# A transformer chain on one core: attention's and the cell's query and key units strictly in turn, with new program orders in the mixers

## The reference

```
proj = h @ w_in                       # aq ak av | mq mk mv mo | gates
aq = partial_rotary(aq) * 64 ** -0.5  # attention: 8 heads of 64
ak = partial_rotary(ak)
attn = dilated_attention_mixture(aq, ak, av)
qk = silu(depthwise_conv5(mq, mk) + conv_b)   # the cell: 4 heads of 128
cell = mlstm(qk, mv, gates, forwards) + mlstm(qk, mv, gates, backwards)
merged = [attn, sigmoid(mo) * rms(cell)]
out = merged @ w_out
```

## Time and profile before

| | |
|---|---|
| median of 3 runs | 2042.23 us (2041.54 to 2042.46) |
| profiled execution, its own time | 2042.36 us |
| its span, first to last instruction | 2040.5 us |
| granted TensorE clock, mean | 0.999 of full speed |
| busy, of the span: PE, DVE, ACT, POOL | 99%, 83%, 50%, 5% |
| first mixer, window | 1227 to 1358 us |
| second mixer, window | 1721.3 to 1852.2 us |

### The profile page before, as it was taken

The page is one execution under the profiler, slowest core; times in us unless marked ns, Lnnn a source line. Parts: engine busy times, 40 slices in busy tenths (PEclk is TensorE's granted clock), DMA queues, the critical chain, the costliest instruction groups (busy, mean ns, idle before and its releaser), DMA issues.

```text
span 2040.5 us, 26105 instructions
## 1 busy us (share of the span) xinstructions
PE 2027.1 (99%) x9966; PEld 1699.8 (83%) x9966; DVE 1698.7 (83%) x2866; ACT 1017.7 (50%) x1204; POOL 110.1 (5%) x228
## 2 busy tenths in 40 slices
PE   9999999999999999999999999999999999999998
PEld 7888878888988888888888889888888888978887
DVE  7888889887579887888889877989888987889986
ACT  5554445445565444554454445854445444675442
POOL 0010011000010000000010000010001000001000
PEclk9999999999999999999999999999999999999999
DMA  8576655756446556566566657356656755536562
GB/s 286 173 236 226 193 179 191 228 187 207 157 152 212 200 186 207 186 211 201 186 207 219 201 168 225 125 159 216 199 190 206 225 196 185 186 124 196 187 200 88
DMA packets 291166, 393.22 MB, mean 193 GB/s; under 512 B 9941, under 2 KB 257061, under 8 KB 290914
## 3 DMA queue, kind: packets, MB, share of 16 engines
q1 hardware_dynamic: 284176, 368.16, 55.5%
q10 hardware_dynamic: 4034, 14.23, 2.1%
q0 software_dynamic: 2832, 9.17, 1.6%
HBM read 390.44 MB, written 2.12 MB: 192 GB/s over the span
## 4 chain that ended last, share of the span: by engine, by line
PE 95%; DVE 2%; ACT 1%; issue 0%; DMA 0%; SPq 0%; POOL 0%; POOLq 0%; ACTq 0%; DVEq 0%
PE psum L602 26%; PE psum L604 26%; PE psum L603 26%; PE psum L626 4%; PE psum L641 2%; PE psum L646 2%; PE psum L650 2%; PE psum L628 2%; PE psum L735 1%; DVE w_lo L1780 1%; PE psum L780 0%; PE psum L781 0%; PE psum L784 0%; ACT w_hi L1277 0%; PE psum L918 0%
## 5 line engine op out<-in xcount | busy, mean ns | idle before, releaser
L1780 DVE TENSOR_TENSOR w_lo<-raw,w_hi 128x2048 fp32r<-128x2048 f32 x349 | 794.3, 2288 | 109.8 <-ACT w_hi L1277 106.5
L1277 ACT ACTIVATE w_hi<-raw 128x2048 fp32r<-128x2048 f32 x349 | 663.3, 1909 | 120.5 <-PE psum L604 85.3
L602 PE MATMUL psum<-w_hi,xT 128*128 128x512 f32 (+1 forms) x1408 | 545.8, 388 | 0.0
L604 PE MATMUL psum<-w_hi,xT 128*128 128x512 f32 (+1 forms) x1408 | 543.4, 386 | 0.0
L603 PE MATMUL psum<-w_lo,xT 128*128 128x512 f32 (+1 forms) x1408 | 543.3, 386 | 0.0
L1830 DVE STREAM_TRANSPOSE h_turned<-h_full 32x128 f32<-32x128 f32 x1408 | 426.6, 303 | 21.1
L602 PEld LDWEIGHTS psum<-w_hi,xT 128*128 128x128 f32 x1408 | 264.6, 188 | 53.3 <-issue 0.8
L604 PEld LDWEIGHTS psum<-w_hi,xT 128*128 128x128 f32 x1408 | 264.5, 188 | 53.4
L603 PEld LDWEIGHTS psum<-w_lo,xT 128*128 128x128 f32 x1408 | 264.5, 188 | 52.4
L602 PE MATMUL psum<-w_hi,h_hi 128*128 128x512 f32 x768 | 300.0, 391 | 0.0
L604 PE MATMUL psum<-w_hi,h_lo 128*128 128x512 f32 x768 | 299.3, 390 | 0.0
(11 more groups left out here) (255 smaller groups left out, 1916.4 us busy)
## 6 DMA issues: line engine op xcount, KB each, us to landing
raw<-in_ffn_w_in SPq DMA_DIRECT2D x176, 512.0 KB, 4.9
raw<-in_ffn_w_gate SPq DMA_DIRECT2D x88, 512.0 KB, 4.0
raw<-in_ffn_w_up SPq DMA_DIRECT2D x88, 512.0 KB, 5.0
raw<-in_ffn_w_down SPq DMA_DIRECT2D x44, 1024.0 KB, 4.9
raw<-in_ffn_w_out SPq DMA_DIRECT2D x44, 1024.0 KB, 4.9
raw<-in_conv_w_in SPq DMA_DIRECT2D x20, 1024.0 KB, 5.3
raw<-in_mix_w_in SPq DMA_DIRECT2D x16, 1024.0 KB, 5.4
raw<-in_mix_w_in SPq DMA_DIRECT2D x24, 512.0 KB, 4.8
```

Of the source, the lines that this page charges most:

```text
L602: pe.matmul(dst, l_hi, r_hi, start=first, stop=False, skip_group_check=loose)
L604: return pe.matmul(dst, l_lo, r_hi, start=False, stop=last, skip_group_check=loose)
L1277: return act.activation(dst, source, ACT.Copy, **kw)
L1780: dve.tensor_tensor(low(u), raw_of(u), f32(high(u)), ALU.subtract).then_inc(lo_ready, 1)
```

## The change

`MIX_UNITS` now has attention's and the cell's units strictly in turn: aq mk ak mq aq mk ak mq. Loads, tap and rotary tables follow from that list. The programs of TensorE, ScalarE and VectorE in the mixer are the same calls in another order (`first_tap` has other numbers, since the cell's units are now 3, 5, 7 and 9). Nothing is added or taken away, and no other stage is touched. The whole diff:

```diff
@@ -111,8 +111,8 @@
 ATTN_UNITS = [("v", 0), ("v", 1), ("v", 2), ("q", 0), ("k", 0), ("q", 1), ("k", 1), ("q", 2), ("k", 2),
               ("q", 3), ("k", 3), ("v", 3)]
 ATTN_PARTS = {"q": 0, "k": 1024, "v": 2048}
-MIX_UNITS = [("av", 0), ("mv", 0), ("aq", 0), ("ak", 0), ("mk", 0), ("mq", 0), ("aq", 1), ("ak", 1),
-             ("mk", 1), ("mq", 1), ("av", 1), ("mv", 1), ("mo", 0), ("mo", 1)]
+MIX_UNITS = [("av", 0), ("mv", 0), ("aq", 0), ("mk", 0), ("ak", 0), ("mq", 0), ("aq", 1), ("mk", 1),
+             ("ak", 1), ("mq", 1), ("av", 1), ("mv", 1), ("mo", 0), ("mo", 1)]
 MIX_CONV_UNITS = [n for n, (part, c) in enumerate(MIX_UNITS) if part in ("mk", "mq")]
 MIX_TURN_UNITS = [n for n, (part, c) in enumerate(MIX_UNITS) if part in ("aq", "ak")]
 MIX_CONVS = [2 * (MIX_UNITS[n][0] == "mk") + MIX_UNITS[n][1] for n in MIX_CONV_UNITS]
@@ -1171,41 +1171,41 @@
                 part_of(3, 0)
                 part_of(3, 1).then_inc(unit_used, 1)
                 running_sums()
+                source_rows()
                 part_of(4, 0)
-                source_rows()
                 part_of(4, 1).then_inc(unit_used, 1)
+                part_of(5, 0)
                 maxima_columns()
                 pair_logits(0)
-                part_of(5, 0)
                 part_of(5, 1).then_inc(unit_used, 1)
                 part_of(6, 0)
+                pair_logits(1)
                 part_of(6, 1).then_inc(unit_used, 1)
                 part_of(7, 0)
                 turn_weights(0)
-                pair_logits(1)
                 part_of(7, 1).then_inc(unit_used, 1)
                 turn_weights(1)
+                key_query(0)
                 part_of(8, 0)
-                key_query(0)
+                part_of(8, 1).then_inc(unit_used, 1)
                 pair_out(0)
-                part_of(8, 1).then_inc(unit_used, 1)
                 turn_weights(2)
                 part_of(9, 0)
                 sums(0)
                 part_of(9, 1).then_inc(unit_used, 1)
                 sums(1)
                 pair_logits(2)
+                key_query(1)
                 turn_weights(3)
-                key_query(1)
                 sums(2)
-                pair_out(1)
                 part_of(10, 0)
                 pair_logits(3)
-                turn_weights(4)
                 part_of(10, 1).then_inc(unit_used, 1)
+                pair_out(1)
                 part_of(11, 0)
                 sums(3)
                 part_of(11, 1).then_inc(unit_used, 1)
+                turn_weights(4)
                 turn_weights(5)
                 key_query(2)
                 part_of(12, 0)
@@ -1607,19 +1607,19 @@
 
                 advance(u + 3)
                 advance(u + 4)
+                advance(u + 5)
                 unit_result(0)
                 gates_out()
                 unit_result(1)
-                advance(u + 5)
                 gate_logs()
                 unit_result(2)
+                unit_result(3)
                 advance(u + 6)
                 advance(u + 7)
+                unit_result(4)
+                first_tap(3)
+                unit_result(5)
                 advance(u + 8)
-                unit_result(3)
-                unit_result(4)
-                first_tap(4)
-                unit_result(5)
                 first_tap(5)
                 exps(0)
                 advance(u + 9)
@@ -1628,51 +1628,51 @@
                 q_or_k(0)
                 q_or_k(1)
                 turned(0)
+                advance(u + 11)
                 unit_result(6)
-                advance(u + 11)
                 turned(1)
-                floors()
                 exps(2)
                 unit_result(7)
+                floors()
+                first_tap(7)
                 decays(0)
                 exps(3)
+                decays(1)
                 advance(u + 12)
-                decays(1)
+                heads_result(0)
                 unit_result(8)
                 turned(2)
-                heads_result(0)
-                first_tap(8)
                 decays(2)
+                decays(3)
                 advance(u + 13)
-                decays(3)
                 unit_result(9)
-                first_tap(9)
                 turned(3)
                 decays(4)
                 exps(4)
                 exps(5)
                 advance(u + 14)
+                first_tap(9)
                 decays(5)
+                q_or_k(2)
+                heads_result(1)
+                decays(6)
+                unit_result(10)
+                q_or_k(3)
                 turned(4)
-                decays(6)
-                heads_result(1)
-                q_or_k(2)
-                q_or_k(3)
-                unit_result(10)
                 first_rows(11)
+                unit_result(11)
                 turned(5)
                 advance(u + 15)
-                unit_result(11)
+                advance(u + 16)
                 decays(7)
                 exps(6)
-                advance(u + 16)
                 exps(7)
                 unit_result(12)
+                turned(6)
                 heads_result(2)
-                turned(6)
                 first_rows(13)
+                unit_result(13)
                 turned(7)
-                unit_result(13)
                 act.wait_ge(in_read, seen.next(in_read, 14))
                 act.activation(out_gate[:], out_gate[:], ACT.Sigmoid).then_inc(g_act, 1)
                 advance(u + 17)
@@ -2194,68 +2194,68 @@
 
                 seen.skip(pads_ready, 1)
                 advance(u + 3)
-                logs()
                 advance(u + 4)
                 advance(u + 5)
+                logs()
+                sources()
                 rotary_position(0)
+                running_maxima()
                 advance(u + 6)
-                sources()
                 rotary_position(1)
-                running_maxima()
                 advance(u + 7)
+                q_or_k_conv(0)
+                mask_exponents(0)
                 attn_logits(0)
-                q_or_k_conv(0)
-                advance(u + 8)
                 attn_logits(1)
                 q_or_k_conv(1)
+                advance(u + 8)
+                advance(u + 9)
                 attn_weights(0)
                 attn_weights(1)
-                advance(u + 9)
-                mask_exponents(0)
+                stabilisers()
+                advance(u + 10)
                 attn_logits(2)
-                advance(u + 10)
-                stabilisers()
+                mask_exponents(1)
+                advance(u + 11)
+                attn_logits(3)
+                attn_weights(2)
+                weights(0)
+                attn_weights(3)
+                weights(1)
                 rotary_position(2)
-                advance(u + 11)
-                mask_exponents(1)
-                attn_weights(2)
-                attn_logits(3)
-                weights(0)
                 rotary_position(3)
-                weights(1)
-                attn_weights(3)
                 head_cell(0)
                 advance(u + 12)
                 head_cell(1)
-                low_of_heads(0)
+                attn_logits(4)
                 weights(2)
                 weights(3)
-                attn_logits(4)
                 head_cell(2)
                 attn_logits(5)
+                advance(u + 13)
                 attn_weights(4)
+                low_of_heads(0)
                 q_or_k_conv(2)
-                advance(u + 13)
                 q_or_k_conv(3)
+                head_cell(3)
+                attn_logits(6)
                 attn_weights(5)
-                attn_logits(6)
+                attn_logits(7)
                 advance(u + 14)
                 weights(4)
+                weights(5)
                 low_of_heads(1)
-                head_cell(3)
-                attn_logits(7)
-                weights(5)
                 advance(u + 15)
                 head_cell(4)
                 attn_weights(6)
+                advance(u + 16)
+                weights(6)
                 attn_weights(7)
                 head_cell(5)
-                weights(6)
-                advance(u + 16)
+                low_of_heads(2)
                 head_cell(6)
                 weights(7)
                 head_cell(7)
-                low_of_heads(2)
 
                 link(dve.tensor_tensor(cell_sq, cell, cell, ALU.mult))
                 dve.tensor_reduce(cell_sum[:], cell_sq.rearrange("p h (d n) -> p h d n", n=P), AX.X,
```

## The result

The changed kernel takes 2052.89 us (median of 4, 2052.79 to 2053.41), the kernel before beside it 2041.88. The ratio is 1.0056, 95% interval 1.0044 to 1.0068. That is 11.0 us more where 9.3 were forecast, inside the range and on the side that was given 0.87.

What follows compares the result with a forecast made beforehand. TensorE, busy 99% of the span, was taken to bound the kernel. Per mixer 4.0 - 0.2 + 0.85 = 4.65 us, for two 9.3, gave 2042.2 + 9.3 = 2051.5 us; range 2045 to 2056.5.

Steps and rivals of the forecast that it cites:

- the side that was given 0.87: Whole kernel: slower by over 0.2%, above 2046.3 us; chance 0.87.
- Unit 7: TensorE starts unit 7 5.1 us later, waiting for VectorE's split; 4.0 us net of pair_logits(1) done meanwhile, per mixer.
- every stall named on the way: TensorE waits before unit 7: behind running sums about 0.5 us, before unit 5 0.6, before pair_logits(1) 1.
- pushes: VectorE idles about 7 us before sources()'s copy, so 4.8 us of its work moves behind 1256.10.
- ScalarE is not in the way: ScalarE's split of unit 7 ends at about 1273, five us before VectorE comes to it.
- `sums(2)`: TensorE's 0.91 us wait for weights(2) shrinks by 0.2 us per mixer; bounds -0.9 to +0.9.
- `turn_weights(4)` and `(5)`: Now side by side on TensorE, the second starting some 1.3 us after the first: +0.85 us per mixer, bounds 0.7 to 1.5.
- nothing covers it: The 0.85 us between the two turns shows in full, since TensorE's queue holds nothing else ahead.
- Table loads: ScalarE makes two more per mixer, 1.28 us each, priced at 2.6 us on ScalarE and nothing on the path.
- Pace of the matmuls: TensorE's matmul runs may go faster or slower after different breaks: at most +/-1.5 us per mixer, likelier half.

Runs made afterwards that it cites:

- gap_filled: Changed kernel with rotary_position(0) and unit 5's split ahead of sources() on VectorE, ScalarE splitting units 5 and 6 before unit 3's result: 2053.81 us, ratio 1.0060.
- work_ahead: gap_filled with unit 6's split and q_or_k_conv(0) ahead of rotary_position(1), unit 7's split ahead of q_or_k_conv(1): 2056.91 us, ratio 1.0076.
- splits_ahead: gap_filled with ScalarE's and VectorE's early programs rewritten so no split of units 5 to 8 queues behind a result: 2046.15 us, ratio 1.0023.
- sources_first_again: splits_ahead with sources() put back directly behind logs(), ahead of rotary_position(0) and unit 5's split on VectorE: 2058.69 us, ratio 1.0086.
- turns_apart: Changed kernel with turn_weights(4) moved ahead of pair_out(1) on TensorE, no longer directly before turn_weights(5): 2052.82 us, ratio 1.0056.
- splits_ahead_late: splits_ahead with the late part eased: turn_weights(4) earlier on TensorE, reordered decays and turn copy on ScalarE, attn_weights(5) earlier on VectorE: 2044.85 us, ratio 1.0018.
- units_alone: Kernel before with only the list of units changed (first_tap renumbered), the three programs as they were: 2064.95 us, ratio 1.0121.
- units_maxima_first: units_alone with running_maxima() moved ahead of rotary_position(1) on VectorE: 2058.65 us, ratio 1.0082.

## Why the prediction was right, and what it had wrong

- **Unit 7.** Forecast 5.1 us late, 4.0 net of the logits moved ahead of it; measured 34.93 - 29.61 = 5.3 and 4.3. The addition of VectorE's list held to 0.3 us, and every stall named on the way is in the trace: 0.47 us behind the running sums (0.5 forecast), 0.47 before unit 5 (0.6), 1.21 before `pair_logits(1)` (1).
- **Its cause.** The prediction has VectorE stand still behind `sources()` and says that this pushes 4.8 us behind the running sums. The idle time is there, 5.75 us, but "pushes" is the step that failed as an explanation: with it filled nothing was gained. Three holds lie one behind the other: `sources()` ahead of ready work; attention's key one unit later, for which `rotary_position(1)` waits; ScalarE's splits queued behind results. The sum had only 0.3 us for the second, because the first covers it, and "ScalarE is not in the way" was true of a VectorE that came late by itself. gap_filled opens the first, work_ahead the first two, and neither gains; splits_ahead opens what held in all three and gains 6.7 of the 11.0 us; sources_first_again closes the first alone and loses more than that, part of it to the clock. That the first hold is enough by itself is shown by sources_first_again, at another place. For the third it is in part argued: work_ahead leaves it as the only one and VectorE is idle for 5.54 us there, but the same edit delays `pair_logits(0)` and the clock falls. The second was never left as the only one, so for it this is not shown.
- **`sums(2)`.** Forecast 0.2 gained; measured a wait of 1.22 where 0.91 was, and 0.06 lost. The bounds (-0.9 to +0.9) hold it.
- **`turn_weights(4)` and `(5)`.** Forecast +0.85 (a distance of 1.3 us); measured a distance of 1.48, +1.04. But "nothing covers it" was wrong as a cause: with the two apart the wait stays, for the queue behind `q_or_k(3)`, inside the bound of the prediction (ScalarE still in `q_or_k(3)`) and not in its value.
- **Table loads.** Two more per mixer, as counted (1208 ScalarE instructions against 1204). One of them does stand in the queue that holds the copy, so they need not have been free; what they cost alone was not measured. The Trainium skill, "ScalarE: Activation LUTs", section "What ACT_TABLE_LOAD costs", puts a drain of 1.38 us on each. The traces disagree here too: in turns_apart the activation at 1319.34 follows the load at 1318.05 after 1.29, and ahead of the load stand only the 0.48 us for VectorE's taps.
- **Not foreseen:** about 0.4 us at `sums(6)`, 0.19 of it a recorded wait for `head_cell`. With the terms above, 4.3 + 0.06 + 1.04 + 0.4 = 5.8 of the 5.85 measured per mixer, where 4.65 was forecast. Twice that is 11.7, the second mixer has 0.16 less, and the stages ahead of the first mixer took 0.9 less in this execution, which leaves the span's 10.7.
- **Pace of the matmuls**, bounded at 1.5 us per mixer: no sign of it in the sum.

Of the new unit order's cost 1.7 us per mixer are left in splits_ahead_late. Whether they belong to the order itself, or to programs that could still be better, stays open. All terms that were mis-sized erred to the same side, so the change cost 1.7 us more than forecast, and the hit owes little to errors that cancel.

## What to carry to other kernels

Before moving a waiting call ahead of ready work, list what is queued behind it on its engine; then ask the same of the next wait, for when one hold is opened the next one in series takes all the gain (4.3 to 5.8 us of VectorE's idle time appeared at three different places). Work that waits for nothing, such as a split whose data has landed, should not be queued behind the copy of a result. And an addition along one engine's program can give the right time while the cause that it seems to name is only one of several in series; only putting the step back into a version without the others shows that it counts.

## What the runs showed of the hardware

- The granted TensorE clock falls to half (1.2 GHz) behind some waits and stays at 2.4 behind others: it fell behind 5.23 us in units_alone, 3.45 in sources_first_again, 3.01 in units_maxima_first and 1.54 in work_ahead; it stayed at 1.00 behind 1.53 in gap_filled and behind 1.77 in the changed kernel. In units_alone the same wait before `sums(1)` did both: 3.04 us without a fall in the first mixer, 3.03 with one in the second. Where it fell in work_ahead, 48 matmuls took 7.3 us instead of 5.7 (1267.2 to 1274.5). So a wait can cost twice its length, its length alone did not tell which, and one kernel can be some us faster or slower from one execution to the next by it.
- A table load stands sometimes before the wait of its activation and sometimes behind. Before the change the load for the gates' exponential ran at 1245.21, ahead of a wait of 0.50; in the changed kernel it began at 1246.13 after a wait of 3.64 us, so that the 1.28 us came on top. Here VectorE's wait for the running sums hides it.
